# Gathering the tokens of two experts together in a mixture-of-experts stage that streams its weights

## The reference

```python
logits = (tokens @ w_router + b_router).astype(jnp.float32)
top_logits, top_idx = lax.top_k(logits, TOP_K)
top_w = jax.nn.softmax(top_logits, axis=-1)
...
    rows = lax.dynamic_slice_in_dim(row_token, j * R, R)
    wts = lax.dynamic_slice_in_dim(row_weight, j * R, R)
    e = block_expert[j]
    hid = tokens[rows] @ w_exp_in[e] + b_exp_in[e]
    out = _clamped_swiglu(hid) @ w_exp_out[e] + b_exp_out[e]
    return out * wts[:, None].astype(out.dtype)
...
y = jnp.zeros((T, D), out.dtype).at[row_token].add(out)
```

## Time and profile before

| what | us |
|---|---|
| median of 3 runs | 2710.94 |
| lowest and highest of them | 2704.83, 2712.97 |
| the profiled execution | 2707.55 |
| its span from first to last instruction | 2705.7 |
| TensorE busy in it | 2587.4 (96%) |
| VectorE, ScalarE busy | 1513.2, 898.6 |
| bytes moved | 704.75 MB, mean 260 GB/s |
| chain that ended last | TensorE 76%, DMA 12%, VectorE 6%, ScalarE 3% |

### The profile page before, as it was taken

How to read it: one execution, slowest core, us unless ns; L and a number is a source line. 1 busy time by engine, 2 the same in 40 slices (tenths; PEclk the granted TensorE clock), 3 DMA queues, 4 the chain that set the end, 5 groups by cost and what they waited for, 6 DMA issues and landing times.

```text
span 2705.7 us, 48950 instructions
## 1 busy us (share of the span) xinstructions
PE 2587.4 (96%) x19460; PEld 2095.8 (77%) x19461; DVE 1513.2 (56%) x2703; ACT 898.6 (33%) x1388; POOL 36.7 (1%) x24
## 2 busy tenths in 40 slices
PE   7999999999899999999979978999999999999998
PEld 6999699999899969999968877965555555555554
DVE  5666666666666666666656786543444434334344
ACT  4434454443444445444434634411111111111111
POOL 0000000000000000000000120000000000000000
PEclk9999999999999989999989998999999999999999
DMA  9644545444444455444534223689999999999997
GB/s 266 238 176 168 210 176 183 157 178 182 155 177 182 166 205 214 178 162 185 186 153 150 104 86 145 233 343 424 430 430 430 430 430 430 430 430 430 430 430 305
DMA packets 70939, 704.75 MB, mean 260 GB/s; under 512 B 11063, under 2 KB 11319, under 8 KB 14343
## 3 DMA queue, kind: packets, MB, share of 16 engines
q1 hardware_dynamic: 65736, 695.11, 63.8%
q0 software_dynamic: 5088, 8.05, 1.4%
HBM read 699.43 MB, written 3.67 MB: 260 GB/s over the span
## 4 chain that ended last, share of the span: by engine, by line
PE 76%; DMA 12%; DVE 6%; ACT 3%; issue 2%; SPq 0%; DVEq 0%; ACTq 0%
PE ps L1630 15%; PE ps L1633 15%; PE ps L1634 15%; DMA slot<-in_experts 12%; PE ps L2142 9%; PE ps L2166 6%; PE ps L2122 4%; PE ps L2179 2%; PE ps L1661 1%; DVE u_lo L981 1%; PE ps L1664 1%; PE ps L1665 1%; PE ps L2152 1%; ACT u_hi L559 1%; DVE acc L1347 1%
## 5 line engine op out<-in xcount | busy, mean ns | idle before, releaser
L981 DVE TENSOR_TENSOR u_lo<-ring,u_hi 128x1024 fp32r<-128x1024 f32 x500 | 615.9, 1237 | 462.1 <-ACT u_hi L559 458.5
L559 ACT ACTIVATE u_hi<-ring 128x1024 fp32r<-128x1024 f32 x498 | 524.1, 1057 | 692.2 <-PE ps L1630 641.5
L1630 PE MATMUL ps<-hs,u_hi 128*128 128x256 f32 x2408 | 694.0, 288 | 24.5 <-DVE hs L1007 22.7
L1633 PE MATMUL ps<-hs,u_hi 128*128 128x256 f32 x2408 | 687.2, 285 | 0.0
L1634 PE MATMUL ps<-hs,u_lo 128*128 128x256 f32 x2408 | 687.0, 285 | 0.0
L1630 PEld LDWEIGHTS ps<-hs,u_hi 128*128 128x128 f32 x2408 | 468.2, 194 | 36.1 <-DVE hs L1007 22.0
L1633 PEld LDWEIGHTS ps<-hs,u_hi 128*128 128x128 f32 x2408 | 468.5, 195 | 0.5
L1634 PEld LDWEIGHTS ps<-hs,u_lo 128*128 128x128 f32 x2408 | 468.1, 194 | 0.0
L2142 PE MATMUL ps<-slot,xg 128*64 128x256 f32 x4032 | 460.9, 380 | 5.9 <-DMA slot<-in_experts 5.9
L2142 PEld LDWEIGHTS ps<-slot,xg 128*64 128x64 f32 x4032 | 287.3, 137 | 211.8 <-issue 66.6
L2166 PE MATMUL ps<-slot,eact 128*64 128x512 f32 x1008 | 244.1, 605 | 0.0
(11 more groups left out here) (356 smaller groups left out, 3038.4 us busy)
## 6 DMA issues: line engine op xcount, KB each, us to landing
slot<-in_experts SPq DMA_DIRECT2D x248, 1536.0 KB, 18.8
ring<-in_stream SPq DMA_DIRECT2D x184, 1536.0 KB, 6.2
extra_in<-in_experts SPq DMA_DIRECT2D x4, 1024.0 KB, 11.8
slot<-in_experts SPq DMA_DIRECT2D x4, 1024.0 KB, 4.8
bias<-bias_rows POOLq DMA_DIRECT2D x2, 1280.0 KB, 11.7
konst<-in_konst POOLq DMA_DIRECT2D x1, 2272.0 KB, 14.8
extra_out<-in_experts SPq DMA_DIRECT2D x4, 512.0 KB, 8.9
slot<-in_experts SPq DMA_DIRECT2D x4, 512.0 KB, 15.1
```

The lines of the kernel that those rows point to most:

```text
L559: nc.scalar.activation(u_hi[buffer_of(l, k)][:, :], raw_unit(l, k), ACT.Copy).then_inc(unit_hi, 1)
L981: nc.vector.tensor_tensor(u_lo[b][:, :], raw_unit(l, kk), u_hi[b][:, :].bitcast(F32), ALU.subtract).then_inc(unit_lo, 1)
L1630: mm = mm_(dst, hi, x_hi, start=first, stop=False, skip_group_check=True)
L1633: mm_(dst, hi, x_lo, start=False, stop=False, skip_group_check=True)
```

## The change

Two neighbouring experts form a couple. Their tokens are gathered by one set of products of 128 columns, and this gather is cut in two halves of four chunks of channels each, one in step 0 and one in step 1 of the couple's predecessor's second expert; both halves use bank 2 (in the first couple, banks 2 and 6). The second half waits until VectorE has taken the first. The places of a couple are found at once, and transposed once per couple, after the second half. ScalarE copies the transposed places to both halves of the partitions with four operations. The loops run over two couples a round. The bias products and their additions move behind the first expert's step 0, into other banks. `wt` gets another place in SBUF, since `xg` and `placeT` need more.

```diff
             def find_places(e):
+
                 for t in range(TT):
-                    op = nc.vector.tensor_scalar(place[:, t, :], count_up, rank[:, t, e:e + 1] if isinstance(e, int) else rank[:, t, bass.ds(e, 1)], None, ALU.is_equal)
+                    for o in range(2):
+                        r = rank[:, t, e + o:e + o + 1] if isinstance(e, int) else rank[:, t, bass.ds(e + o, 1)]
+                        op = nc.vector.tensor_scalar(place[:, t, o * CAP:(o + 1) * CAP], count_up[:, 0:CAP], r, None, ALU.is_equal)
                 op.then_inc(place_ready, 1)
...
+            def take_places(q, w):
+
+                a.wait_ge(placeT_ready, q + 1)
+                for o in range(2):
+                    for h in range(2):
+                        copy = nc.scalar.activation(placeT[w][h * CAP:(h + 1) * CAP, o, :], ps[o * CAP:(o + 1) * CAP, 5, 0:TOK], ACT.Copy)
+                copy.then_inc(placeT_taken, 1)
...
+            def take_tokens(q, half, w, bank=2):
+
+                v.wait_ge(xg_ready, q * 2 + (half + 1))
+                part, chunks = xg[w][:, half * PAIRS:(half + 1) * PAIRS, :], slice(half * PAIRS, (half + 1) * PAIRS)
...
-                if j == 1 and not last:
-                    take_tokens(p, e + 1, 1 - b)
+                if odd and j < 2 and not last:
+                    take_tokens(q + 1, j, (i // 2 + 1) % 2)
...
-            def gather(n, first=False):
-
-                pe.wait_ge(place_ready, n + 1)
-                for c in range(DC):
+            def gather(q, half, bank=2, first=False):
+
+                pe.wait_ge(place_ready, q + 1)
+                if not first:
+                    pe.wait_ge(xg_taken, q * 2 + half)
+                for c in range(PAIRS):
+                    at = (half * PAIRS + c) * P
                     for t in range(TT):
-                        mm = mm_(ps[:, 2, c * CAP:(c + 1) * CAP], h_tok[:, t, c * P:(c + 1) * P], place[:, t, 0:CAP], start=t == 0, stop=t == TT - 1)
+                        mm = mm_(ps[:, bank, c * 2 * CAP:(c + 1) * 2 * CAP], h_tok[:, t, at:at + P], place[:, t, :], start=t == 0, stop=t == TT - 1)
                 mm.then_inc(xg_ready, 1)
...
-                if j == 1 and not last:
-                    gather(n + 1)
+                    back(n - 1, q + (odd - 1), (i - 1) % 4, j)
+                if odd and j < 2 and not last:
+                    gather(q + 1, j)
+                    if j == 1:
+                        turn_places(q + 1)
...
             def bias_sums():
 
                 pe.wait_ge(wtT_taken, 1)
                 pe.wait_ge(bout_scaled, 1)
-                pe.wait_ge(rows_taken, 4)
+                pe.wait_ge(placeT_taken, 1)
...
-                gather(n, first=True)
+                gather(p * COUPLES, 0, first=True)
+                gather(p * COUPLES, 1, bank=6, first=True)
+                turn_places(p * COUPLES, first=True)
+                if isinstance(p, int):
+                    pe.wait_ge(rows_taken, 4)
+                expert_in(p, 0, 0, 0, 0)
+                expert_in(p, 0, 0, 0, 1)
+                turn(n, 0, first=True)
+                expert_step(p, 0, 0, 0, 0, first=True)
                 if isinstance(p, int):
                     bias_sums()
-                expert_in(p, 0, 0, 0)
-                pe.wait_ge(ybias_taken, 2 * TT)
...
+                expert_step(p, 0, 0, 0, 1, first=True)
+                if isinstance(p, int):
+                    pe.wait_ge(ybias_taken, 2 * TT)
+                for i in range(4):
+                    expert_turn(p, i, i // 2, i)
+                with pe.Fori(1, EXPERTS // 4 - 1) as g:
+                    for i in range(4):
+                        expert_turn(p, g * 4 + i, g * 2 + i // 2, i)
```

More of the change, by code:

```diff
@@ L923, in take_hidden, with expert_step @@
                 nc.scalar.activation(hid_tok[:, j % 2, :], ps[:, j % 2, 0:2 * P], ACT.Copy).then_inc(htok_copied, 1)
-            def expert_step(n, j, b, last=False):
+            def expert_step(n, q, i, j, last=False):
                 a.wait_ge(glu_ready, n * PAIRS + (j + 1))
@@ L1510, in _, with couple_steps, expert_step @@
             before_experts = step.base + step.k + 2
[L1512 to L1525, removed]
-                moe.base, moe.k = before_experts + p * (EXPERTS * MOE_STEPS + 1) + 1 + e * MOE_STEPS, 2 * j + (1 if j > 1 and not last else 0)
+            def couple_steps(p, ql):
+                return before_experts + p * (COUPLES * COUPLE_STEPS + 1) + ql * COUPLE_STEPS
+            def take_tokens(q, half, w, bank=2):
+                v.wait_ge(xg_ready, q * 2 + (half + 1))
+                part, chunks = xg[w][:, half * PAIRS:(half + 1) * PAIRS, :], slice(half * PAIRS, (half + 1) * PAIRS)
+                gain, shift = modgain[:, DC:2 * DC][:, chunks], mod[:, 3 * DC:4 * DC][:, chunks]
+                moe(nc.vector.tensor_tensor(part, ps[:, bank, :].rearrange("p (a b) -> p a b", b=2 * CAP),
+                                            gain.unsqueeze(2).to_broadcast([P, PAIRS, 2 * CAP]), ALU.mult))
+                nc.vector.tensor_tensor(part, part, shift.unsqueeze(2).to_broadcast([P, PAIRS, 2 * CAP]), ALU.add).then_inc(xg_taken, 1)
+            def expert_step(p, e, ql, i, j, after=True, places=True, last=False):
+                n, q = p * EXPERTS + e, p * COUPLES + ql
+                odd = i % 2
+                moe.base, moe.k = couple_steps(p, ql) + 2, odd * 2 * PAIRS + 2 * j + (0 if last or not odd else min(j, 2))
                 v.wait_ge(turned, n * PAIRS + (j + 1))
@@ L1565, in expert_pass @@
                 n = p * EXPERTS
-                take_tokens(p, 0, 0, after_first=False)
+                moe.base, moe.k = couple_steps(p, 0), 0
+                take_tokens(p * COUPLES, 0, 0)
+                take_tokens(p * COUPLES, 1, 0, bank=6)
+                expert_step(p, 0, 0, 0, 0, after=False)
+                expert_step(p, 0, 0, 0, 1, after=False)
                 if isinstance(p, int):
@@ L2130, in gather, with expert_in @@
                 mm.then_inc(placeT_ready, 1)
-            def expert_in(p, e, j, b):
-                if j == 0:
-                    pe.wait_ge(xg_taken, p * EXPERTS + e + 1)
+            def expert_in(p, e, ql, i, j):
+                own = slice(i % 2 * CAP, (i % 2 + 1) * CAP)
                 for k in range(2):
+                    if j == 0 and i % 2 == 0:
+                        pe.wait_ge(xg_taken, p * EXPERTS + ql * 2 + (k + 1))
                     wait_tile(pe, p, e, 2 * j + k)
@@ L2178, in back, with expert_step @@
                     rows = slice(h * CAP, (h + 1) * CAP)
[L2179 to L2182 removed]
+                    mm_(ps[:, banks[h], :], placeT[i // 2][rows, i % 2, t * P:(t + 1) * P], outd[rows, :], start=True, stop=True).then_inc(scat_ready, 1)
+            def expert_step(p, e, ql, i, j, first=False, last=False):
+                n, q, odd = p * EXPERTS + e, p * COUPLES + ql, i % 2
                 if j + 2 < PAIRS:
[L2184 removed]
+                    expert_in(p, e, ql, i, j + 2)
                 elif not last:
[L2186 removed]
+                    expert_in(p, e + 1, ql + odd, (i + 1) % 4, j + 2 - PAIRS)
                 if j < 2 and not first:
[L2188 to L2190 removed]
+                    back(n - 1, q + (odd - 1), (i - 1) % 4, j)
[3 more added lines that the diff above has]
+                        turn_places(q + 1)
                 if j + 1 < PAIRS:
```

131 lines of the change are left out of this document (59 added, 72 removed).

## The result

Four runs each on one chip: before 2709.99 us (2704.83 to 2712.97), after 2733.9 us (2733.06 to 2736.25). The ratio is 1.0094, 95% interval 1.0082 to 1.0107: the change costs 24 us, where 3.4 us were to be gained. The profiled execution took 2734.68 us with a span of 2732.8, at a mean granted clock of 0.981, as before (0.980).

What follows compares the result with a forecast made beforehand. The weight stream at 430 GB/s was taken to bound the kernel, only TensorE's work before 1818.77 us setting the end. Terms -7.65 + 3.84 + 0.13 + 0.3 = -3.4 gave 2710.94 - 3.4 = 2707.5 us, range 2700 to 2713.5.

Steps and rivals of the forecast that it cites:

- the part on the stream: Weight loads at the experts' stage start: issued 1.6 and 3.4 us earlier, so all 3.4 us reaches the end.
- the sum: TensorE's work ahead of `moe_used` 11: -7.65 + 3.84 + 0.13 + 0.3 = -3.4 us.
- The waits, the queues and the gather: Stage start: new waits hidden, loads 1.6 and 3.4 us earlier, half gather 1.92 us at 0.12 a record.
- the stretch at half clock: TensorE's low clock around 1763 to 1770 us: it stays, and other work filling it loses the same.
- The bias products: Moved behind the second expert step's start: 2.02 us at half clock, about 1.0 at full; the move worth 0.
- The end: End of the kernel: 3.4 us earlier, through shorter DMA idle time after the loop's first loads.
- TensorE's catching up: Experts' loop: TensorE's period near 27 us until it catches the stream, sooner than 2222 us, then 29.26.
- (A): The wide gather costs twice, or a new wait holds TensorE 3 us before 1818: gain 0, 2707.6 us; 0.08 with (E).
- (E): Gathers only regrouped, with as many records: the change doesn't do what it says, outcome as (A); 0.08 with (A).
- (B): At the stage start the half-clock stretch goes away: 3.3 us more, so -6.7; chance 0.05.
- (C): The loop's TensorE saving is real time: 57 us less, 2651 us; chance 0.01.
- (D): TensorE idles in the loop, its clock is low when the last tile lands: +9.8, 2717.4 us; 0.06, half in full.

Runs made afterwards that it cites:

- the experiment: The kernel before, with TensorE's and ScalarE's loops written over four experts a round and VectorE's left at two: 2748.0 us, ratio 1.0153.

## Why the prediction was wrong

**The step that failed** is in the part on the stream, "all of the 3.4 us reaches the end": it took from rows of before that the stream keeps 430 GB/s behind 1822 us, and the sum has no term for the form of the loops, though the diff shows rounds growing from two experts to four on three engines. I had asked of every moved operation what it costs, but not of the loops what their length costs. The term is +27.7 us: after costs 23.9 us against its runs of before, and the same change with a short VectorE loop gains 3.8 against its own. The long loop put alone into the kernel before measures the term a second time, without the rest of the change: 28.0 us. The forecast gain and this term give -3.4 + 28.0 = +24.6, where +23.9 was measured.

**Where the loss arises.** 30 packets of code more than in the version with the short loop, 0.9 us of stream for each; the kernel before with the long loop alone gives 28 us for 29 packets. 8 KB take 0.02 us at the 430 GB/s of all sixteen DMA engines, but a packet of code is carried by one of them, and takes 0.31 us there in the trace of after (a weights packet of 12 KB 0.46). If the stream goes by the engine that lags, this is its least price, a third to a half of what the runs show; for the rest there is no row. The lagging engine explains two things more. At first the loss is not seen in the rate: from 1900 to 2150 us still 429 GB/s are moved, while TensorE consumed tiles at 4 x 12.58 MB / 121.5 us = 414. Fifteen engines ran ahead of the tiles' completion, and the ten microseconds at the end are what is left of this lead; that the slots then bounded it, and the rate fell, is argued. And the DMA share falls by less than the bytes, from 1.01 to 0.99 where they fall from 430 to 411 GB/s.

**The waits, the queues and the gather** were right. Chain of after: a half gather takes 1.98 us for 16 records (0.12 each, as the earlier trace rows had said) where 1.92 was forecast; the places cost 0.75 us instead of 0.48, +0.27 for a forecast 0.3. Against the start of the places (1760.16; before 1760.32) the output products that set `moe_used` 9 and 11 come 2.1 and 3.8 us earlier, forecast 1.6 and 3.4. The 0.4 more is not in the sum; the stretch at half clock lies over other work now. None of the new waits shows in the chain before 1818 us.

**The bias products** were worth what was said, little or nothing: they take 1.07 us at full clock instead of 2.02, and in after the clock is again granted at 0.50 for six to seven microseconds (now from 1760 to 1767 us), while the first gather runs (6.46 us instead of 4.98).

**The end** of the sum was right in sum and sign once the loop is undone: -3.8 us by the medians, -3.05 by the profiled executions, for -3.4. The idle time of the DMA engines was shortened, as forecast, not removed: from 1760 to 1830 us their share was 0.84 before and is 0.90 in after. (Two loads from 1807.8 us on, at 3.66 us each, are moved by 1815.1 us, not 1816.2 as the prediction has it; the next was to be issued later than either, so nothing hangs on it.)

**TensorE's catching up** came sooner than 2222 us, as forecast: the chain waits for a tile from 1917.22 on. But the period then was 30.4 us, not 29.26, which is the row on which the forecast broke.

**The rivals.** (A) and (E) fell with the gather's records. (B) did not happen in after, but it does happen without the change. In the profiled executions of the version with the short loop and of the kernel with VectorE's loop written out, the granted clock is 1.00 all through 1756 to 1776 us. In the latter, whose TensorE program is that of before, the first load of the loop comes 46.88 us after the start of the stage instead of 49.11. So a start at full clock is worth 2.2 us, not the 3.3 of the prediction; it comes and goes with the execution, and a part of a gain of 3 to 4 us in one pair of profiled executions can be this luck. The medians of 11 and 15 runs are the safer figure. (C) fell: TensorE's loop got shorter and the stream gave nothing back. (D) had the right sign by the wrong cause. TensorE waited for tiles 72 times in 1800 to 2680 us, 71.4 us in all and 2.3 us at most. After one of the longest of these waits the clock did fall to its lower level:

```profile
2015.69 3.63 PE L2163 MATMUL ps<-slot,xg 128*64 128x256 f32 x16 [2.26 <-DMA slot<-in_experts]
```

```profile
2016.00:2019.00 3.00, 3.00 (x16) 1.47 (x12) 1.82 (x9) 0.31 (x1) 0.00 (x0) 0.50 1.05 441
```

The 16 records took 3.63 us instead of 1.9, and it cost the end nothing, as the prediction had said of a fall in the loop; in the windows of 1900 to 2150 and 2222 to 2480 us the mean clock is 0.99 and 1.00, and from 2704 to 2712 us, when the last tile lands, it is 1.00. The Trainium skill (TensorE: Matmul & The Clock Gate, "HAM oscillation") describes a loop in which each wait for a tile is longer than the work ahead of it, and in which the clock falls every time. The loop here is not of that form: its waits are 1.0 us on the average, with several microseconds of work between them, and from 1830 to 2710 us the clock fell this once.

**A rule that bore on it.** The Trainium skill (Runtime: NRT & Kernel Launch, "Instruction fetch mechanics") says that each engine keeps a small part of its program at hand, and that a branch back to code outside it stalls the engine while the DMA brings it. Put beside the diff, it would have been a rival of its own. The trace agrees with it on the stall (4.5 us on VectorE, 3.1 to 4.6 on TensorE in the experiment). By its figure of 512 instructions for VectorE the round of 294 would have fitted; the runs show that it is fetched again all the same. Its blocks of 16 KB appear on TensorE's queue alone, while VectorE's and GpSimd's measure 8 KB.

**What stays open**: why a block of 8 KB costs 0.6 us (VectorE's straight line) to 1.0 us (VectorE's loop) of the stream, when it occupies an engine for 0.31; how much of the latter is the standstill; why four to five blocks come for a round of 294 instructions; and where exactly the limits lie.

## What to carry to other kernels

Count the instructions in a loop's round on each engine before and after a change of its form, and look at the packets of the instruction queues in the stretch: a round that outgrows the engine's instruction memory is paid for anew in each round. Where the DMA engines are full, that traffic costs even if the engine that fetches is idle (24 us here for 0.37 MB of code on GpSimd), and in the stage where their share was 0.34 it cost nothing. Then look at the end of a stream: a DMA share that stands at one sixteenth is one engine that lags. If a loop needs alternating buffers, address them by a register rather than by writing out more turns.

## What the hardware showed that I had not expected

- VectorE: a round of 149 to 151 listed instructions stays loaded; one of 293 or 294 is fetched again each time, with a standstill of 4.5 to 5.1 us. TensorE: 438 listed instructions stay, 470 don't, with standstills of 3.1 to 4.6 us. (Those that only wait for a semaphore are not counted.)
- Code arrives in packets of 8 KB for VectorE and GpSimd (0.57 MB in 69 packets on q14) and of 16 KB for TensorE (0.98 MB in 60 on q8). While the weights stream, GpSimd pauses after most blocks of 128 instructions, 0.2 to 1.1 us; with the DMA engines at 0.34 it went through 1337 without a pause.
- A stream at 430 GB/s loses 0.6 to 1.0 us for each such packet of 8 KB, 30 to 50 times what its bytes take at that rate and two to three times what the packet takes on its engine (0.31 us).
- One DMA engine of sixteen ends five to ten microseconds after the others where loaded code slowed the stream, and under 3 us after them in the kernel before.
- The busy share of the DMA engines hardly shows it: 0.99 at 411 GB/s, 1.01 at 430.
- After a wait for a tile of 2.26 us TensorE's granted clock was 0.50 for 3 us.
